# First loads issued one behind another, the bias product moved behind the first chunk, and the rotated score products of a head pair put in one group

## The chip, the cores and the metric

One Trainium2 chip, one of its cores. The metric is the device time of one execution in microseconds (us), as the median of several runs. The work is in fp32 accuracy: each fp32 weight tile is cut into a high and a low part, and each product of the large layers is done as three products of parts.

## The reference

Two transformer blocks over 256 tokens of width 1024. What matters here is the very start and the first attention, a latent attention (MLA) with 8 heads:

```python
h = x @ w_in                                  # 384 query, 256 key/value, 64 rotary columns
c_q  = _rmsnorm(h[..., :384], g_q)
c_kv = _rmsnorm(h[..., 384:640], g_kv)
k_r = _rope(h[..., 640:], pos)
q = einsum('bsr,rhd->bshd', c_q, w_uq)
q_n, q_r = q[..., :128], _rope(q[..., 128:], pos)
...
s = (q_n . k_n  +  q_r . k_r) * scale         # causal, per head; 128 plus 64 deep
p = softmax(s)
...
```

The second attention (sliding window, 16 heads of depth 64) adds a relative bias to its scores. After it come MLPs, a recurrence, a stick-breaking attention, a memory attention and a convolutional FFN. They are not touched.

## The kernel before

The program is written out by hand for each engine, with semaphores between them.

All large weights come as one stream of 319 slots of 512 KB. SyncE (SP) loads slot n into `raw[:, n % 4]`. ScalarE makes the high part `whi` (line 1472), VectorE subtracts to get the low part `wlo` (line 2093), and TensorE uses both. A `raw` buffer is loaded anew when its `wlo` is made (`cut_lo`). ScalarE and VectorE cut three slots ahead of TensorE (`AHEAD = 3`): slots 0, 1 and 2 before the loop, and slot j + 3 at the head of its turn j.

At the start SP issues slots 0 to 3 without a wait. ScalarE issues from its own queue, in this order: the first two of eight feature chunks of x (`x_loaded`), the other six (`x_rest_loaded`), the first 1025 columns of the table `con` (identity, ones, causal mask, cosine and sine), and the parameters `par`. GpSimd issues `relb` and the band rows (`band_loaded`). Then ScalarE copies the first pair of chunks of x to `xh`, cuts slot 0, copies the other three pairs and cuts slots 1 and 2. VectorE follows with `xl` (signal `x_cut`, one count for a pair), `wlo` of slot 0, the other three pairs, and `wlo` of slots 1 and 2. Then VectorE works on `par`, reads the bias product's result (`brow`), waits for `con_loaded`, and goes on with the chunks of ("in", j).

TensorE's queue starts with 28 products of a tile of zeros, each 128 x 512 bf16. Then comes the bias product `brow` (32 deep, 16 wide, 384 columns), which waits for the band rows. Then come the chunks ("in", 0) to ("in", 2). A chunk is 8 tiles of one slot against 256 tokens, in 24 products (lines 701, 704, 705). ("in", 0) waits at tile k for `x_cut`. Then `kvstat`, ("in", 3) to ("in", 5), keys, and the list `MLA_PE`, which fixes the order of the latent attention:

```python
MLA_PE = [("g", 0), ("r", 0), ("n", 0), ("r", 1), ("n", 1), ("n", 2), ("n", 3), ("s", 0), ("s", 1), ("v", 0), ("t", 0), ("t", 1), ("s", 2),
          ("v", 1), ("t", 2), ("t", 3), ("o", 0), ("o", 1), ("s", 3), ("w", 0), ("t", 4), ("t", 5), ("w", 1), ("o", 2), ("o", 3),
```

("s", n) is the scores of heads 2n and 2n + 1. ("v", n) and ("w", n) are gathers of twelve products of 512 columns. ("t", h) is the transposes of head h's probabilities (line 926), and ("o", h) the output. For the scores, VectorE takes scaled maxima, ScalarE the exponentials, and VectorE the normalised probabilities in `sc` and `pr` (even and odd heads), line 2288. VectorE's order is scores of pair 0, normalise head 0, scores of pair 1, normalise head 1.

In ("s", n) the latent part multiplies the full height of the array (128 rows, `qn` by `kn`, line 961). The rotated part (`qr` by `kr`, line 963) is 64 deep: head 2n uses the low half of the array's rows and head 2n + 1 the high half. Query tokens 0 to 127 see keys 0 to 127 (128 columns), and tokens 128 to 255 see all 256. These operands are plain fp32, and each such product is run in two passes. The second attention's scores (line 1044) are half-height products alone: for a pair of heads 128 columns low and high, then 256 columns low and high.

The four `work` banks of PSUM are handed to results in the order of the list `RESULTS`, result n in bank n % 4.

Of the kernel before, what the change touches and what calls it, by code (L numbers as in the profile page):

```python
# [24 lines left out]
P = 128  # L25
T = 256
# [13 lines left out]
RING = 4  # L40
# [26 lines left out]
CCOL = {}  # L67
# [149 lines left out]
def _results(stage, names):  # L217
    RESULTS.extend((stage, n) for n in names)


_results("brow", [0])
_results("in", range(3))
_results("kvstat", [0])
_results("in", range(3, 6))
_results("k", range(4))
# [83 lines left out]
def build(nc, w, xt, x_tok, ln_rows, memt, mem_tok, consts_in, band_in, params_in, lora_in, gate2_in, relb_in, out):  # L309
    ctx = ExitStack()  # L310
    with ctx:
# [8 lines left out]
        raw = tensor(ctx, "raw", [P, RING, 1024])  # L320
        whi = tensor(ctx, "whi", [P, RING, 1024], F32R)
        wlo = tensor(ctx, "wlo", [P, RING, 1024], F32R)
        con = tensor(ctx, "con", [P, NCON])
# [7 lines left out]
        xh, xl = xhl[:, 0, :, :], xhl[:, 1, :, :]  # L331
# [17 lines left out]
        with ExitStack() as first:  # L349
# [14 lines left out]
            kr = tensor(first, "kr", [P, T])  # L364
            qr = tensor(first, "qr", [P, 4, T])
            nsink = tensor(first, "nsink", [P, 16])
            qlat = tensor(first, "qlat", [P, 8, 2 * T])
            qn, kn = qlat[:, 0:4, :], qlat[:, 4:8, :]
# [54 lines left out]
        work = [ctx.enter_context(nc.psum_tensor(f"work{b}", [P, 512], F32)) for b in range(4)]  # L423
# [36 lines left out]
        def of_head(tile, h):  # L460
            return tile[:, h // 2, h % 2 * T:h % 2 * T + T]
# [81 lines left out]
        HALVES = (LOW, HIGH)  # L543
# [7 lines left out]
        raw_loaded = [sem(f"raw_loaded{r}") for r in range(RING)]  # L551
# [7 lines left out]
        def sig(name):  # L559
            if name not in named:  # L560
                named[name] = sem(name)
            return named[name]
# [27 lines left out]

        @block.sync
        def _(sp):
            for n in range(RING):
                sp.dma_start(raw[:, n, :], w[n]).then_inc(raw_loaded[n], 16)
            rounds = NSLOT // RING
            for n in range(RING, 3 * RING):
                sp.wait_ge(cut_lo, n + 1 - RING)
                sp.dma_start(raw[:, n % RING, :], w[n]).then_inc(raw_loaded[n % RING], 16)
                if n == RING + 2:
                    sp.dma_start(memraw[:, :, :], memt).then_inc(sig("mem_loaded"), 16)  # L600
                elif n == 2 * RING + 2:
                    sp.dma_start(x[:, :, :], mem_tok).then_inc(sig("mem_tok_loaded"), 16)
            with sp.Fori(3, rounds) as i:
                for r in range(RING):

                    sp.wait_ge(cut_lo, i * RING + (r + 1 - RING))
                    sp.dma_start(raw[:, r, :], w[bass.ds(i * RING + r, 1), :, :].rearrange("a p n -> p (a n)"))\
                        .then_inc(raw_loaded[r], 16)
            for n in range(rounds * RING, NSLOT):
                sp.wait_ge(cut_lo, n + 1 - RING)  # L610
                sp.dma_start(raw[:, n % RING, :], w[n]).then_inc(raw_loaded[n % RING], 16)
            for b in range(4):
                sp.wait_ge(sig("final"), b + 1)
                sp.dma_start(tok(out, b // 2, b % 2), tok(rest, b // 2, b % 2)).then_inc(sig("stored"), 16)
            sp.wait_ge(sig("stored"), 64)
# [65 lines left out]
        def _(pe):  # L681
            mm = nc.tensor.matmul
# [42 lines left out]
            def chunk(stage, j, key, hi, lo, waits=None):  # L725

                n = SLOT[stage] + j
                bank = open_result(key)
                slot_start(n)
                for k in range(DC):  # L730
                    if waits is not None:
                        waits(k)
                    last = cut_product(bank[:, 0:T], n, k, hi[:, k, :], lo[:, k, :], k == 0, k == DC - 1, k == 0)
                close_result(last, key)
# [46 lines left out]
            def zero_products(bank, count):  # L781


                for _ in range(count):
                    mm(bank[:, :], zeros[:, :], mask4(zeros[:, :]), start=True, stop=True)
# [109 lines left out]


            pe.wait_ge(sig("zeros_set"), 1)
            zero_products(work[3], 28)
            pe.wait_ge(sig("band_loaded"), 32)
            close_result(mm(open_result(("brow", 0))[0:16, 0:384], relb[:, :], bandt[:, 0, :], start=True, stop=True), ("brow", 0))  # L900
            for j in range(3):
                chunk("in", j, ("in", j), xh, xl, (lambda k: pe.wait_ge(sig("x_cut"), k // 2 + 1)) if j == 0 else None)
            pe.wait_ge(sig("con_loaded"), 16)
            bank = open_result(("kvstat", 0))
            pe.wait_ge(sig("in_sq"), 2)
            for j in range(2):
                last = mm(bank[:, 0:T], ones, hsq(j), start=j == 0, stop=j == 1)
# [4 lines left out]
            for p in range(4):  # L912
                bank = open_result(("k", p))
                for e in range(2):
                    for c in range(2):
# [3 lines left out]
                        last = cut_product(bank[:, e * T:(e + 1) * T], SLOT["uk"] + s, tile, ckvh[:, c, :], ckvl[:, c, :], c == 0, c == 1, tile == 0)  # L919
# [11 lines left out]
            for kind, n in MLA_PE:  # L931
                key = ("mla", (kind, n))
                if kind == "g":
                    bank = open_result(key)
                    pe.wait_ge(sig("in_sq"), 5)
                    for t in range(2):
                        for j in range(3):
                            last = mm(bank[:, 32 * t:32 * t + 32], hsq(2 + j)[:, half(t)], C("ones", 1).broadcast_to([P, 32]), start=j == 0, stop=j == 2)
                    close_result(last, key)
                elif kind == "v":  # L940
                    gather("v", SLOT["uv"] + n, ckvh[:, n, :], ckvl[:, n, :], n == 0, n == 1)
                elif kind in "rn":
                    bank = open_result(key)
                    for e in range(2):
                        for k in range(3):
                            s, tile = divmod(MLA_TILE[(kind, n)] + 3 * e + k, 8)
                            if tile == 0:
                                slot_start(SLOT["q"] + s)
                            last = cut_product(bank[:, e * T:(e + 1) * T], SLOT["q"] + s, tile, cqh[:, k, :], cql[:, k, :], k == 0, k == 2, tile == 0)
                    close_result(last, key)  # L950
                elif kind == "s":

                    keys = [("mla", ("s", 2 * n + e)) for e in range(2)]
                    banks = [open_result(k) for k in keys]
                    wait_drained(pe, ("k", n))
                    wait_drained(pe, ("mla", ("n", n)))
                    pe.wait_ge(sig("kr_ready"), 1)
                    pe.wait_ge(sig("qr_ready"), n // 2 + 1)
                    for cols_, q, width in ((slice(0, P), 0, P), (slice(P, 3 * P), P, T)):
                        for e, bank in enumerate(banks):  # L960
                            mm(bank[:, cols_], of_head(qn, 2 * n + e)[:, q:q + P], of_head(kn, 2 * n + e)[:, 0:width], start=True, stop=False)
                        for e, bank in enumerate(banks):
                            last = mm(bank[:, cols_], qr[HALVES[e], n, q:q + P], kr[HALVES[e], 0:width], start=False, stop=True)
                            if q:
                                close_result(last, keys[e])
                elif kind == "t":
                    transposes("mla", n, [(0, 0), (1, 1), (2, 2)])
                elif kind == "o":
                    bank = open_result(key)
                    wait_drained(pe, ("mla", ("t", n)))  # L970
                    pe.wait_ge(sig(f"v_kept{n // 4}"), 2)
                    mm(bank[:, 0:T], rest[:, 0, n * VD:(n + 1) * VD], pT[:, n % 4, 0:T], start=True, stop=False)
                    last = mm(bank[:, P:T], rest[:, 1, n * VD:(n + 1) * VD], pT[:, n % 4, T:3 * P], start=False, stop=True)
                    close_result(last, key)
                else:
                    wait_drained(pe, ("mla", ("o", n)))
                    gather("wo", SLOT["wo"] + n, oh[:, n, :], ol[:, n, :], n == 0, n == DC - 1)
# [56 lines left out]
            for kind, h in SWA_ALL:  # L1034
                key = ("swa", (kind, h))
                if kind == "s":

                    keys = [("swa", ("s", 2 * h + e)) for e in range(2)]
                    banks = [open_result(k) for k in keys]
# [11 lines left out]
                elif kind == "o":  # L1051
                    bank = open_result(key)
# [57 lines left out]
            for t in range(2):  # L1110
                bank = open_result(("vtok", t))
# [348 lines left out]
        def _(act):  # L1460
# [49 lines left out]

            act.dma_start(sqr[:, 0:2, :], xt[:, 0:2, :]).then_inc(sig("x_loaded"), 16)
            act.dma_start(sqr[:, 2:DC, :], xt[:, 2:DC, :]).then_inc(sig("x_rest_loaded"), 16)
            first_con = CCOL["blockones"]
            act.dma_start(con[:, 0:first_con], consts_in[:, 0:first_con]).then_inc(sig("con_loaded"), 16)
            act.dma_start(par[:, :], params_in).then_inc(sig("par_loaded"), 16)

            def table(func, src=None):
# [1403 lines left out]
```

## Time and profile before

| | us |
|---|---|
| median of 3 runs | 1075.38 (1075.04 to 1075.98) |
| the profiled execution | 1074.92 |
| its span | 1073.1 |
| TensorE busy with products | 1063.8 |
| VectorE busy | 781.5 |
| ScalarE busy | 642.5 |

The span runs from the first to the last instruction of the profile; 1.8 us of the execution lie around it. Times of instructions are counted from the span's start. Products (PE) are pipelined and their ends are modelled, so the distance between two starts says more than one duration. PEld is the loading of weights into the array, DVE is VectorE, ACT is ScalarE, and SPq, ACTq and POOLq are the issuing of transfers. The time to landing of a transfer counts from its issue.

### The profile page before, as it was taken

The page shows a single profiled execution, that of the slowest core. Times are in us where ns is not written, and L with a number is a line of the kernel's source. Part 1 is how long each engine was busy: PE and PEld are TensorE (multiplying, and loading weights), DVE is VectorE, ACT ScalarE, POOL GpSimd, SP SyncE. Part 2 cuts the span into 40 slices and gives each one's busy share as a digit, 9 for nine tenths or more (in the row PEclk, how much of TensorE's full clock was granted, in tenths as well). Part 3 has the DMA queues.
Part 4 walks back from the last instruction along what each step waited for, and adds up shares of the span by engine and source line. Part 5 has one row for each costly group of instructions (what it writes and reads, how often), then busy time and mean ns, then how long its engine had stood idle before and what let it go on. Part 6 is the DMA issues. An engine that isn't in the chain of part 4 may idle for free.

```text
span 1073.1 us, 21320 instructions
## 1 busy us (share of the span) xinstructions
PE 1063.8 (99%) x7745; PEld 931.8 (87%) x7745; DVE 781.5 (73%) x1370; ACT 642.5 (60%) x1160; POOL 15.0 (1%) x29
## 2 busy tenths in 40 slices
PE   9999999999999999999999999999999999999998
PEld 7978888888887788888888988898999979999997
DVE  5877766667896676666687888656764968877776
ACT  5876555544676765445568974445567357666663
POOL 1000000000000000000010000000000000000000
PEclk9999999999999999999999999999999999999999
DMA  8636555555665346555564543122255645656662
GB/s 323 248 133 216 190 184 194 195 184 170 213 216 155 103 156 197 189 182 181 190 221 135 175 136 103 49 76 76 80 177 176 180 155 178 196 180 191 183 190 97
DMA packets 49170, 181.75 MB, mean 169 GB/s; under 512 B 5537, under 2 KB 5697, under 8 KB 48209
## 3 DMA queue, kind: packets, MB, share of 16 engines
q1 hardware_dynamic: 46800, 170.41, 48.8%
q0 software_dynamic: 1584, 7.63, 2.4%
q10 hardware_dynamic: 720, 2.79, 0.7%
q8 instruction: 46, 0.75, 0.3%
q14 instruction: 20, 0.16, 0.1%
HBM read 179.74 MB, written 1.07 MB: 168 GB/s over the span
## 4 chain that ended last, share of the span: by engine, by line
PE 86%; DVE 8%; ACT 3%; issue 1%; DMA 1%; ACTq 0%; DVEq 0%
PE acc L774 25%; PE work L717 8%; PE work L701 7%; PE work L704 7%; PE work L705 7%; PE work L720 4%; PE acc L701 4%; PE acc L705 3%; PE acc L704 3%; DVE wlo L2093 3%; ACT whi L1472 2%; PE work L722 1%; PE work L757 1%; DMA sqr<-x_t 1%; PE work L926 1%
## 5 line engine op out<-in xcount | busy, mean ns | idle before, releaser
L2093 DVE TENSOR_TENSOR wlo<-raw,whi 128x1024 fp32r<-128x1024 f32 x317 | 382.5, 1223 | 87.1 <-ACT whi L1472 85.2
L1472 ACT ACTIVATE whi<-raw 128x1024 fp32r<-128x1024 f32 x319 | 335.4, 1058 | 50.1 <-PE work L701 18.9
L701 PE MATMUL work<-xhl,whi 128*128 128x256 f32 x544 | 154.4, 284 | 0.9 <-ACT k_ L1818 0.2
L704 PE MATMUL work<-xhl,whi 128*128 128x256 f32 x544 | 152.7, 281 | 0.0
L705 PE MATMUL work<-xhl,wlo 128*128 128x256 f32 x544 | 152.7, 281 | 0.0
L717 PE MATMUL work<-xhl,whi 128*128 128x512 f32 x420 | 148.9, 393 | 0.0
L720 PE MATMUL work<-xhl,wlo 128*128 128x256 f32 x480 | 124.7, 280 | 0.0
L774 PE MATMUL acc<-whi,hh 128*128 128x512 f32 x344 | 109.6, 396 | 0.7 <-DVE hl L2108 0.7
L774 PE MATMUL acc<-whi,hl 128*128 128x512 f32 x344 | 109.0, 395 | 0.0
L774 PE MATMUL acc<-wlo,hh 128*128 128x512 f32 x344 | 108.9, 395 | 0.0
L701 PEld LDWEIGHTS work<-xhl,whi 128*128 128x128 f32 x544 | 102.5, 188 | 5.4 <-DVE sm L2272 1.6
L704 PEld LDWEIGHTS work<-xhl,whi 128*128 128x128 f32 x544 | 102.5, 188 | 1.1 <-issue 0.2
L705 PEld LDWEIGHTS work<-xhl,wlo 128*128 128x128 f32 x544 | 102.6, 189 | 0.0
L720 PEld LDWEIGHTS work<-xhl,wlo 128*128 128x128 f32 x480 | 90.4, 188 | 5.0
L717 PEld LDWEIGHTS work<-xhl,whi 128*128 128x128 f32 x420 | 78.9, 188 | 17.9
L701 PE MATMUL acc<-xhl,whi 128*128 128x256 f32 x288 | 86.2, 299 | 0.0
L1712 ACT ACTIVATE ha<-work 128x256 f32<-128x256 f32 x64 | 24.6, 384 | 94.3 <-PE work L717 91.6
L704 PE MATMUL acc<-xhl,whi 128*128 128x256 f32 x288 | 80.8, 281 | 0.0
L705 PE MATMUL acc<-xhl,wlo 128*128 128x256 f32 x288 | 80.8, 281 | 0.0
L774 PEld LDWEIGHTS acc<-wlo,hh 128*128 128x128 f32 x344 | 64.5, 187 | 15.8
L774 PEld LDWEIGHTS acc<-whi,hl 128*128 128x128 f32 x344 | 64.5, 188 | 15.6
L774 PEld LDWEIGHTS acc<-whi,hh 128*128 128x128 f32 x344 | 63.3, 188 | 12.7 <-DVE hl L2108 1.5
(464 smaller groups left out, 1900.5 us busy)
## 6 DMA issues: line engine op xcount, KB each, us to landing
raw<-weights SPq DMA_DIRECT2D x319, 512.0 KB, 3.7
gb<-ln_rows POOLq DMA_DIRECT2D x4, 1024.0 KB, 6.7
memraw<-mem_t SPq DMA_DIRECT2D x1, 1024.0 KB, 7.2
x<-mem_tok SPq DMA_DIRECT2D x1, 1024.0 KB, 5.8
x<-x_tok ACTq DMA_DIRECT2D x1, 1024.0 KB, 6.6
qlat<-bias_scratch POOLq DMA_DIRECT2D x1, 1024.0 KB, 11.1
qlat<-bias_scratch POOLq DMA_DIRECT2D x4, 256.0 KB, 4.3
out_tok<-res SPq DMA_DIRECT2D x4, 256.0 KB, 2.1
```

Source lines behind the costliest of these rows:

```text
L701: a = mm(dst, whi[:, n % RING, col], hi, start=start, stop=False, skip_group_check=shared)
L704: mm(dst, whi[:, n % RING, col], lo, start=False, stop=False, skip_group_check=shared)
L705: return mm(dst, wlo[:, n % RING, col], hi, start=False, stop=stop, skip_group_check=shared)
L717: a = mm(two_halves(bank), whi[:, n % RING, col], xhl[:, :, k, :], **both)
L720: last = mm(bank[:, 0:T], wlo[:, n % RING, col], xh[:, k, :], start=False, stop=False, skip_group_check=True)
L722: last = mm(two_halves(bank), whi[:, n % RING, col], xhl[:, :, k, :], **both)
L757: last = mm(banks[j][:, 0:T], whi[:, (n + j) % RING, k * P:k * P + P], xl[:, k, :], start=False, stop=k == DC - 1)
L774: ins = mm(acc[2 * t + d][:, :], left[:, half(t)], right[:, n % RING, d * 512:d * 512 + 512], start=first and a == 0, stop=last and a == 2)
L926: last = nc.tensor.transpose(bank[:, b * P:b * P + P], probability_buffer(stage, h)[:, a * P:a * P + P], C("ident"))
L1472: act_fn(whi[:, n % RING, :], raw[:, n % RING, :], ACT.Copy).then_inc(cut_hi, 1)
L1712: act_fn(ha[:, f % 2, :], bank[:, T:2 * T] if f >= 2 or it is not None else bank[:, 0:T], ACT.Copy).then_inc(sig("up_low"), 1)
L2093: tt(wlo[:, n % RING, :], raw[:, n % RING, :], whi[:, n % RING, :].bitcast(F32), ALU.subtract).then_inc(cut_lo, 1)
```

## The change

- SP issues slot 0 at once, slot 1 when the first part of x has landed, slot 2 when the rest of x has landed, slot 3 when slot 1 has landed, and then, when slot 2 has landed, the first columns of `con`, which ScalarE issued before.
- TensorE runs 31 products of zeros instead of 28, and the bias product comes behind ("in", 0) instead of ahead of it. The list of results follows, so ("in", 0) has bank 0 and the bias product bank 1.
- In the latent scores of a head pair the four latent products come first (head by head, 128 then 256 columns), and the four rotated products stand together behind them. The first product of a bank starts it, and those of its other columns don't.

```diff
-_results("brow", [0])
-_results("in", range(3))
+_results("in", [0])
+_results("brow", [0])
+_results("in", range(1, 3))
...
-            for n in range(RING):
-                sp.dma_start(raw[:, n, :], w[n]).then_inc(raw_loaded[n], 16)
+            sp.dma_start(raw[:, 0, :], w[0]).then_inc(raw_loaded[0], 16)
+            sp.wait_ge(sig("x_loaded"), 16)
+            sp.dma_start(raw[:, 1, :], w[1]).then_inc(raw_loaded[1], 16)
+            sp.wait_ge(sig("x_rest_loaded"), 16)
+            sp.dma_start(raw[:, 2, :], w[2]).then_inc(raw_loaded[2], 16)
+            sp.wait_ge(raw_loaded[1], 16)
+            sp.dma_start(raw[:, 3, :], w[3]).then_inc(raw_loaded[3], 16)
+            sp.wait_ge(raw_loaded[2], 16)
+            first_con = CCOL["blockones"]
+            sp.dma_start(con[:, 0:first_con], consts_in[:, 0:first_con]).then_inc(sig("con_loaded"), 16)
...
-            zero_products(work[3], 28)
+            zero_products(work[3], 31)
+            chunk("in", 0, ("in", 0), xh, xl, lambda k: pe.wait_ge(sig("x_cut"), k // 2 + 1))
             pe.wait_ge(sig("band_loaded"), 32)
             close_result(mm(open_result(("brow", 0))[0:16, 0:384], relb[:, :], bandt[:, 0, :], start=True, stop=True), ("brow", 0))
-            for j in range(3):
-                chunk("in", j, ("in", j), xh, xl, (lambda k: pe.wait_ge(sig("x_cut"), k // 2 + 1)) if j == 0 else None)
+            for j in range(1, 3):
+                chunk("in", j, ("in", j), xh, xl)
...
-                    for cols_, q, width in ((slice(0, P), 0, P), (slice(P, 3 * P), P, T)):
+                    tiles = ((slice(0, P), 0, P), (slice(P, 3 * P), P, T))
+                    for e, bank in enumerate(banks):
+                        for cols_, q, width in tiles:
+                            mm(bank[:, cols_], of_head(qn, 2 * n + e)[:, q:q + P], of_head(kn, 2 * n + e)[:, 0:width], start=q == 0, stop=False,
+                               skip_group_check=True)
+                    for cols_, q, width in tiles:
                         for e, bank in enumerate(banks):
-                            mm(bank[:, cols_], of_head(qn, 2 * n + e)[:, q:q + P], of_head(kn, 2 * n + e)[:, 0:width], start=True, stop=False)
-                        for e, bank in enumerate(banks):
-                            last = mm(bank[:, cols_], qr[HALVES[e], n, q:q + P], kr[HALVES[e], 0:width], start=False, stop=True)
+                            last = mm(bank[:, cols_], qr[HALVES[e], n, q:q + P], kr[HALVES[e], 0:width], start=False, stop=q > 0,
+                                      skip_group_check=True)
                             if q:
                                 close_result(last, keys[e])
...
-            first_con = CCOL["blockones"]
-            act.dma_start(con[:, 0:first_con], consts_in[:, 0:first_con]).then_inc(sig("con_loaded"), 16)
             act.dma_start(par[:, :], params_in).then_inc(sig("par_loaded"), 16)
```

## Rows read from the trace of the kernel before

**Rows 1.** The page's busy time, share of the span and instructions.
```profile
PE 1063.8 (99%) x7745; PEld 931.8 (87%) x7745; DVE 781.5 (73%) x1370; ACT 642.5 (60%) x1160; POOL 15.0 (1%) x29
```

**Rows 2.** TensorE's waits from 0 to 100 us: total, times, longest.
```profile
PE work L701 <- DVE wlo L2093: 0.2, 1, 0.2
```

**Rows 3.** Chain that ended last, first 60 us: start, us, what.
```profile
1.19 9.13 DMA sqr<-x_t
10.34 1.67 ACT xhl L1585 x3
12.02 0.96 ACT whi L1472
...
14.28 0.38 PE work L701
```

**Rows 4.** Timeline of TensorE's weight loads, first 11 us: start, duration, instruction.
```profile
1.41 0.15 PEld L785 LDWEIGHTS work<-zeros 128*128 128x128 bf16 x1 [0.28 <-issue]
...
6.50 2.90 PEld L785 LDWEIGHTS work<-zeros 128*128 128x128 bf16 x14 [0.25 <-issue]
9.91 0.11 PEld L900 LDWEIGHTS work<-qlat,relb 32*16 32x16 f32 x2 [0.50 <-DMA qlat<-band_rows]
10.65 0.19 PEld L701 LDWEIGHTS work<-xhl,whi 128*128 128x128 f32 x1 [0.64 <-issue]
```

**Rows 5.** Timeline of TensorE's products, from 8.5 us and to 17.3 us.
```profile
8.23 1.67 PE L785 MATMUL work<-zeros 128*128 128x512 bf16 x7
...
13.86 0.28 PE L705 MATMUL work<-xhl,wlo 128*128 128x256 f32 x1
...
17.21 0.28 PE L701 MATMUL work<-xhl,whi 128*128 128x256 f32 x1
```

**Rows 6.** Timeline of VectorE, first 13 us.
```profile
7.99 1.23 DVE L2093 TENSOR_TENSOR wlo<-raw,whi 128x1024 fp32r<-128x1024 f32 x1 [0.25 <-ACT whi L1472]
11.01 1.89 DVE L2108 TENSOR_TENSOR xhl<-sqr,xhl 128x512 fp32r<-128x512 f32 x3 [1.79 <-ACT xhl L1585]
```

**Rows 7.** Windows: busy of each engine, then PEclk, DMA share, GB/s.
```profile
1.00:8.00 7.00, 6.99 (x20) 2.63 (x21) 0.70 (x2) 3.07 (x4) 1.29 (x4) 1.00 0.86 271
```

**Rows 8.** Transfers: issued near 0.7, near 2.4 and near 14.3 us.
```profile
sqr<-x_t ACTq DMA_DIRECT2D x1, 256.0 KB, 5.5
...
raw<-weights SPq DMA_DIRECT2D x1, 512.0 KB, 12.0
...
raw<-weights SPq DMA_DIRECT2D x1, 512.0 KB, 3.5
```

**Rows 9.** TensorE's products of ("s", 0), merged and in narrow stretches.
```profile
49.14 0.60 PE L961 MATMUL work<-qlat 128*128 128x128 f32 x4
49.47 0.28 PE L961 MATMUL work<-qlat 128*128 128x128 f32 x1
49.68 0.49 PE L963 MATMUL work<-kr,qr 64*128 64x128 f32 x4
49.89 0.28 PE L963 MATMUL work<-kr,qr 64*128 64x128 f32 x2
...
51.79 0.71 PE L961 MATMUL work<-qlat 128*128 128x128 f32 x4
```

**Rows 10.** TensorE's products of the second attention's first score group.
```profile
310.07 0.93 PE L1044 MATMUL work<-ks,qlat 64*128 64x128 f32 x8
310.93 0.39 PE L701 MATMUL work<-xhl,whi 128*128 128x256 f32 x1
```

**Rows 11.** Timelines of ScalarE, VectorE and the weight loads, 51 to 58 us.
```profile
51.66 1.28 ACT L1644 ACT_TABLE_LOAD   x1 [0.42 <-ACT x L1667]
...
52.81 0.16 DVE L2278 TENSOR_TENSOR sm<-sm,cols 128x2 f32<-128x2 f32 x1
...
57.02 0.35 DVE L2288 TENSOR_SCALAR pr<-pr,sm 128x256 f32<-128x256 f32 x1
...
57.67 0.14 PEld L926 LDWEIGHTS work<-con,pr 128*128 128x128 f32 x1
```

## The prediction, made blind

> **What bounds the kernel now.** I read the page first: TensorE is busy 1063.8 us of a span of 1073.1 [rows 1]. The reader should take from this that only two kinds of edit can pay: one that lets TensorE start its real work earlier, or one that shortens its own queue. Next I read its waits from 0 to 100 us: but for the one on the zeros tile at the very start there is one, 0.2 us for VectorE's `wlo` [rows 2]. The chain of waits tells where that comes from [rows 3]: the second transfer of x lands at 10.3, ScalarE copies it in three pieces (1.67), cuts slot 1 (0.96), VectorE subtracts it, and ("in", 1) begins at 14.28. From there the chain is TensorE alone for a long way, so its queue from 14.28 on moves as a whole: whatever makes ("in", 1) begin earlier, and whatever shortens the scores at 49 to 68 us, is kept, unless another engine has too little room behind it. Last I read single instructions around the start, the scores and the softmax.
>
> **The start, before.** The weight loads of the zero products come 0.425 us apart up to 6.10 (twelve rows from 1.41), then 14 in 2.90 us, 0.213 apart [rows 4]. 512 columns in these spacings are 1.2 and then 2.4 GHz, though the window view gives a granted clock of 1.00 [rows 7]; I go by the spacings. The last product begins at 8.23 + 6 x 0.213 = 9.51 and has streamed at 9.72 [rows 5]. The bias product waits for the band rows until 9.91 and the first weight load behind it comes at 10.65, 0.74 later [rows 4]. ("in", 0) then ends at 13.86 + 0.12 = 13.98 [rows 5]; it holds 24 products, which without a wait take 17.21 - 14.28 = 2.93 with the first load exposed, 2.82 with it hidden [rows 3, 5].
>
> **The start, after.**
> - Three more zero products: 3 x 0.213 = 0.64, all in TensorE's queue, so they end at 9.72 + 0.64 = 10.36.
> - ("in", 0) follows at once. It needs the first pair of x and `wlo` of slot 0. VectorE ends the latter at 7.99 + 1.23 = 9.22 [rows 6], from two transfers that go out as before; the zeros cover it.
> - x in full: the held loads leave 0.52 (slot 0), 1.05 (x), 0.17 (parameters) and 0.10 MB (band), 1.84 MB, in the queues. From 1 to 8 us the engines moved 7 us x 271 GB/s = 1.90 MB [rows 7], so x is in at about 8.0 instead of 10.3. ScalarE's copies run 8.0 to 9.7 [rows 3], VectorE's three subtractions behind slot 0, 1.89 in all [rows 6], 9.2 to 11.1. They are wanted at 11.1, 11.8 and 12.5, and there by 9.9, 10.5 and 11.1. No wait, where before ("in", 0) lost 13.98 - 10.65 - 2.93 = 0.40. End 10.36 + 2.82 = 13.18.
> - The bias product between two chunks: 0.74 as before plus a change of the array's shape on the way in, 0.1 (the gap at 49.6, below) = 0.84; bounds 0.74 and, with a whole change at 0.21, 0.95. ("in", 1) begins at 14.02. Nothing else waits long for this product: VectorE reaches its result after cut 2, at about 14.3, and now finds it ready at 13.9.
> - Slot 1: SP sits in its wait until the first x pair lands, 0.74 + 5.5 = 6.24 [rows 8], and issues then. The one slot load issued near 14 us, into nearly empty queues, took 3.5; the first x pair, with others beside it, 5.5 [rows 8]. I take 3.5, because only 0.7 MB is ahead of it, moving during its own start-up: in at 9.8, cut by ScalarE at 10.8 (0.96 in [rows 3]), subtracted at 12.1 (1.23 in [rows 6]); by the 5.5 in at 11.7 and subtracted at 14.0. Covered, by 1.9 us or just so.
> - Behind SP's new waits stand slots 2 and 3, the table `con` and slots 4 on. By the same 3.5: slot 2 issued 8.0, in 11.6, subtracted by 14, wanted one chunk after ("in", 1), 14.02 + 2.93 = 16.95. Slot 3 issued 9.8, in 13.3, wanted after 19.8. `con` issued 11.6, in at 15.1 (17.1 at 5.5); VectorE asks for it near 15 and TensorE near 19.8. Slot 4 is issued near 12.1, in by about 17, wanted after 22.6. Removing `con` from ScalarE's queue only brings `par` forward. All at nothing; the cover is the lead of three slots, and `con` becomes the next thing late if it lands after about 17.
>
> So ("in", 1) moves from 14.28 to 14.02: 0.26 us earlier, set by zeros, ("in", 0) and the bias product, no longer by a transfer.
>
> **The scores.** Each of four head pairs runs 2 full products of 128 columns, 2 half-height ones, 2 full of 256, 2 half-height, each in two passes. Pair 0 takes 51.79 - 49.14 = 2.65 [rows 9]. Passes stand 0.107 apart for 128 columns, 0.213 for 256. The last full pass begins at 49.47, should end at 49.58, and the half-height load comes at 49.68: 0.10 lost. Its second pass begins at 49.89 instead of 49.79: 0.11 more, the exposed load. So one change of shape costs 0.21 [rows 9]. After the change a pair has 8 full passes, 4 x 0.107 + 4 x 0.213 = 1.28, then 0.10, then one group of four half-height products of 128 and 256 columns. Such a group stands in the second attention, same shapes and order: 310.93 - 310.07 = 0.86 [rows 10]. New pair 2.24, saved 0.41, which is two changes at 0.21. Four pairs: 1.64. Nothing is added; both results of a pair close at its end as before.
>
> The Trainium skill ("TensorE: Matmul & The Clock Gate", Part 3, The mechanism) says that a weight load overlaps products in flight only when its row group differs; in the group of four the later loads meet their own half. By it three more loads to a half would be exposed, 3 x 0.107 = 0.32, and a pair would save 0.41 - 0.32 = 0.1. The rows disagree with it [rows 10]: there these loads cost nothing.
>
> **What the softmax gives back.** Before the transposes of head 1 only the gather ("v", 0) lies between them and pair 1, and both pairs are shortened: 0.82. Their load comes at 57.67; VectorE ends the probabilities at 57.02 + 0.35 = 57.37 [rows 11]; less about 0.05 for the signal, 0.25 of room. What does that row hang on? ScalarE loads its table until 51.66 + 1.28 = 52.94, and VectorE ends the scaled maximum of head 0 at 52.81 + 0.16 = 52.97 [rows 11]; the first exponential needs both: earlier scores help only by 0.05, since the table load stands behind ScalarE's own queue (the squares of `x`), which moves with the 0.26 alone. So of 0.82 only 0.30 arrives; 0.52 becomes a wait at head 1. Pairs 2 and 3 have each a whole gather and further products between them and their own transposes, and keep 0.41.
>
> **Sum.** 0.26 + 0.30 + 0.82 = 1.38 us off TensorE's queue, and so off the end: the span 1073.1 becomes 1071.7. The profiled execution took 1074.92, 1.8 more than its span and 0.5 less than the median, 1075.38; the median becomes 1074.0.
>
> **Rivals.**
> - **The softmax keeps up** (0.14): the first exponential would have to move with the scores. For it speaks that table and maximum end 0.03 apart; against, that the table comes last. 0.26 + 1.64 = 1.90: 1073.5.
> - **The fast rate comes sooner** (0.12). Zeros now set the start directly, and the step at 6.5 us is set by nothing in the code. Each us sooner saves 0.5, until slot 0 at 9.2 is the bound: at most 1.14 more. 1.38 + 1.14 = 2.5: 1072.9.
> - **The start brings nothing** (0.12): step 1 us later (0.5 lost) or the bias product at 0.95. Gain 0.8 to 1.1: 1074.3 to 1074.6.
> - **Loads of the same half are not hidden** (0.05): each pair saves 0.1, in all 0.26 + 0.4 = 0.66: 1074.7. The second attention speaks against it [rows 10]. It is what the quoted rule of the Trainium skill would give.
> - **Slot 1 late, slower** (0.07). It is issued 5 us later than before. ("in", 1) begins 2.3 after it lands (cut 0.96, subtraction 1.23, signals). The gain of the scores, 1.12, is used up when ("in", 1) begins at 15.4, slot 1 landing at 13.1, 6.9 after issue; over 0.2% slower from 15.3, 9.0 after issue. The last load of the first batch took 12.0 [rows 8]: so priced it lands at 18.2, ("in", 1) begins at 20.5, net 20.5 - 14.28 - 1.12 = 5.1, 1080.5. Against it: that one had some 4 MB around it, this 0.7.
>
> **How the numbers follow.** The forecast has 0.50, its own range 1073.5 to 1074.5. About 0.2%, 2.15 us, is what a measurement tells here from no change. Faster by more (under 1073.2): all of the sooner rate, nearly half of the softmax rival, 0.02 of the forecast, 0.20. Slower: 0.06, slot 1. Same: 0.74. Range: 1072.8 holds the sooner rate down to its bound, 1075.1 the two small-gain rivals; outside remain some 0.05 below and 0.08 above.
>
> **What would show it.** Right: no wait inside ("in", 0), x in near 8, ("in", 1) first product near 14.0, one bias product of about 0.8 ahead of it, eight half-height passes in one row of 0.9, pairs of 2.24, and a new TensorE wait of about 0.5 on VectorE's `pr` near 57. Wrong: a wait on slot 1 or x in the first 20 us, zeros whose fast spacing begins elsewhere than at 6.5, a half-height group over 1 us, or transposes of head 1 that don't wait.

## The result, and the profile after

| | before | changed |
|---|---|---|
| median of 20 runs | 1074.87 us | 1077.18 us |
| lowest to highest | 1074.54 to 1076.83 | 1074.10 to 1079.40 |
| profiled execution | 1074.92 | 1076.10 |
| its span | 1073.1 | 1074.3 |

The ratio of changed to before is 1.0014, with a 95% interval of 1.0007 to 1.0020. It goes by the means (1076.65 and 1075.11); the medians stand 2.3 us apart. The kernel became slower, and its runs spread over 5 us where those of before spread over 2. The profiled execution is one of the better half. It shows 1.2 us of the loss.

The 20 executions fall into two groups, and the granted clock tells them apart. The granted clock is TensorE's clock as a share of its full 2.4 GHz. In 8 executions its mean was 1.000, and they took 1074.10 to 1076.10 (median 1074.5, no slower than before). In the other 12 it was 0.998 or 0.996, and they took 1076.75 to 1079.40 (median 1077.8). In the executions of the kernel before that ran beside the experiments it was never under 0.999. The profiled one belongs to the first group. The fourth set of experiments below has a profile of the second kind, and shows what lowers the mean.

TensorE's waits from 0 to 100 us, for [rows 2]:

```profile
PE work L710 <- DVE ckvl L2120: 1.1, 1, 1.1
...
PE work L917 <- ACT pT L1620: 0.8, 1, 0.8
PE work L936 <- DVE pr L2300: 0.3, 1, 0.3
```

The third is the one that the prediction wanted at head 1. The first two are new and were not in it: the first key product waits for the low part of the latent, and the statistics product for ScalarE's square of ("in", 1). The chain that ended last says where the first comes from, for [rows 3]:

```profile
1.19 7.73 DMA sqr<-x_t
8.93 4.50 DMA raw<-weights
13.45 0.33 SPq L603
13.82 0.43 SPq L607
14.29 7.42 DMA raw<-weights
21.79 1.03 issue
22.82 0.38 ACT ha L1608
...
24.39 0.42 DVE ha L2231
...
30.54 0.70 DVE ckvl L2120
31.29 0.38 PE work L710
```

The reader should follow it from the top. x lands at 8.9, slot 2 is issued then and lands at 13.4, and only then does SP issue the table (L603) and the slots behind it (L607). Slot 5, issued at 14.29, lands at 21.7. ScalarE cuts it ahead of the rotation of chunk 2, VectorE's long line from there ends in `ckvl`, and TensorE waits until 31.29. ScalarE's timeline shows four waits for slots (1.63, 0.43, 2.77 and 1.36), where before it had one of 0.28:

```profile
8.94 1.68 ACT L1597 ACTIVATE xhl<-sqr 128x512 fp32r<-128x512 f32 x3 [1.02 <-DMA sqr<-x_t]
10.76 1.06 ACT L1486 ACTIVATE whi<-raw 128x1024 fp32r<-128x1024 f32 x1
13.45 1.06 ACT L1486 ACTIVATE whi<-raw 128x1024 fp32r<-128x1024 f32 x1 [1.63 <-DMA raw<-weights]
14.95 1.06 ACT L1486 ACTIVATE whi<-raw 128x1024 fp32r<-128x1024 f32 x1 [0.43 <-DMA raw<-weights]
15.91 0.36 ACT L1620 ACTIVATE pT<-work 128x256 f32<-128x256 f32 x1
19.04 1.06 ACT L1486 ACTIVATE whi<-raw 128x1024 fp32r<-128x1024 f32 x1 [2.77 <-DMA raw<-weights]
20.01 0.36 ACT L1620 ACTIVATE pT<-work 128x256 f32<-128x256 f32 x1
21.73 1.06 ACT L1486 ACTIVATE whi<-raw 128x1024 fp32r<-128x1024 f32 x1 [1.36 <-DMA raw<-weights]
```

The square at 20.01 is the one that the statistics product needs. Chunk 1 was finished near 16.8; the square stands behind the cut of slot 4, which lands at 19.0. VectorE meanwhile waits for the table, which lands at 17.8:

```profile
17.83 1.22 DVE L2105 TENSOR_TENSOR wlo<-raw,whi 128x1024 fp32r<-128x1024 f32 x1 [1.25 <-DMA con<-table]
```

The transfers, issued at 6.27 (slot 1), 10.75 (slot 3), 13.45 (table) and 13.82 (slot 4), for [rows 8]; the last number is the time to landing. Slot 2, issued at 8.93, took 4.5 too:

```profile
raw<-weights SPq DMA_DIRECT2D x1, 512.0 KB, 4.5
...
raw<-weights SPq DMA_DIRECT2D x1, 512.0 KB, 4.2
...
con<-table SPq DMA_DIRECT2D x1, 512.5 KB, 4.4
...
raw<-weights SPq DMA_DIRECT2D x1, 512.0 KB, 5.2
```

And the windows from 8 to 15 us, of before and then of the changed kernel. The last two numbers are the engines' share and GB/s:

```profile
8.00:15.00 7.00, 6.71 (x41) 4.45 (x40) 5.11 (x6) 4.38 (x6) 0.00 (x0) 1.00 0.96 367
```

```profile
8.00:15.00 7.00, 7.00 (x46) 5.10 (x45) 4.75 (x6) 3.85 (x6) 0.00 (x0) 1.00 0.76 237
```

In these 7 us the changed kernel moved 7 us x (367 - 237) GB/s = 0.9 MB less, nearly two slots. The start of TensorE's queue did improve, for [rows 4, 5]:

```profile
6.10 3.77 PEld L794 LDWEIGHTS work<-zeros 128*128 128x128 bf16 x18 [0.28 <-issue]
9.99 0.19 PEld L710 LDWEIGHTS work<-xhl,whi 128*128 128x128 f32 x1
```

```profile
13.11 0.81 PE L910 MATMUL work<-qlat,relb 32*16 32x384 f32 x2
13.86 0.39 PE L710 MATMUL work<-xhl,whi 128*128 128x256 f32 x1
```

The second chunk begins at 13.86 against 14.28. The scores, for [rows 9]:

```profile
51.20 1.47 PE L972 MATMUL work<-qlat 128*128 128x128 f32 x8
52.60 0.93 PE L976 MATMUL work<-kr,qr 64*128 64x128 f32 x8
53.46 1.58 PE L972 MATMUL work<-qlat 128*128 128x128 f32 x8
```

A pair takes 53.46 - 51.20 = 2.26. So the difference in time, changed minus before, runs like this: -0.42 at the second chunk; +0.50 at the statistics product (20.52 against 20.02); +1.96 at the first key product (31.29, 29.33); +2.06 at the scores (51.20, 49.14); +1.05 behind them (first gather of the output, 69.32 against 68.27); +1.2 at the end. The scores gave 1.0; between the second chunk and them the start took 2.5.

### The profile page after: what moved, and what is told of

Same layout as the page of the kernel before. It is cut to its first block, busy times and chain, and to the rows that moved or that the text cites. A ratio compares the mean times of both kernels' runs of the same rounds, so it can differ in the third digit from the quotient of the medians.

```text
span 1074.3 us, 21326 instructions
## 1 busy us (share of the span) xinstructions
PE 1063.1 (99%) x7748; PEld 931.8 (87%) x7748; DVE 781.7 (73%) x1370; ACT 641.2 (60%) x1160; POOL 14.9 (1%) x29
## 4 chain that ended last, share of the span: by engine, by line
PE 84%; DVE 8%; ACT 4%; DMA 2%; issue 2%; ACTq 0%; SPq 0%; DVEq 0%
PE acc L783 25%; PE work L726 8%; PE work L710 7%; PE work L713 7%; PE work L714 7%; PE work L729 4%; PE acc L710 4%; PE acc L714 3%; PE acc L713 3%; DVE wlo L2105 3%; ACT whi L1486 2%; DMA raw<-weights 1%; PE work L731 1%; PE work L766 1%; DMA sqr<-x_t 1%
## 5 line engine op out<-in xcount | busy, mean ns | idle before, releaser
L1486 ACT ACTIVATE whi<-raw 128x1024 fp32r<-128x1024 f32 x319 | 335.2, 1057 | 56.3 <-PE work L710 19.6
L726 PEld LDWEIGHTS work<-xhl,whi 128*128 128x128 f32 x420 | 78.9, 188 | 17.9
```

Of the source, the lines that this page charges most:

```text
L726: a = mm(two_halves(bank), whi[:, n % RING, col], xhl[:, :, k, :], **both)
L1486: act_fn(whi[:, n % RING, :], raw[:, n % RING, :], ACT.Copy).then_inc(cut_hi, 1)
```

## The experiments

Each kernel below was run 8 to 11 times beside the kernel before. Ratios are to that kernel, with a 95% interval.

**First set: the parts.** `free_loads` is the changed kernel with its load parts undone.

```diff
-            sp.dma_start(raw[:, 0, :], w[0]).then_inc(raw_loaded[0], 16)
-            sp.wait_ge(sig("x_loaded"), 16)
...
+            for n in range(RING):
+                sp.dma_start(raw[:, n, :], w[n]).then_inc(raw_loaded[n], 16)
...
+            act.dma_start(con[:, 0:first_con], consts_in[:, 0:first_con]).then_inc(sig("con_loaded"), 16)
```

> The changed kernel with the first loads as they were: SP issues slots 0 to 3 without a wait, and ScalarE issues the first part of the constant table. Zeros, bias product and scores stay changed. Theory 1 (the held loads run with pauses between them, the constant table lands near 18 and slot 4 at 19 instead of 13 and 15.6, and ScalarE and VectorE then stand in their queues): both new waits of TensorE are gone, at the statistics product (0.8) and at the first key product (1.1), and the time is about 1.4 below the kernel before, 1073.3 to 1073.9, with a spread between runs as small as before's (about 1). Rival (the order of the bias product and of the result banks makes the waits): they stay, and the time stays near 1076 to 1078.

Measured 1074.38 (1074.19 to 1075.52), ratio 0.9997 (0.9988 to 1.0006). Both waits are gone, so is most of the spread, and the mean granted clock is 1.000 in all 11 executions: theory 1 holds for the waits, and its rival falls. But the gain is 0.4, not 1.4, and the time lies outside the expected range. In its place a wait inside the first chunk appears:

```profile
PE work L702 <- DVE xhl L2114: 1.1, 1, 1.1
```

x lands at 10.3 as before, so the first chunk stands for it, and the bias product comes on top, behind it.

`scores_alone` is the kernel before with the third part of the change alone.

```diff
-                    for cols_, q, width in ((slice(0, P), 0, P), (slice(P, 3 * P), P, T)):
+                    tiles = ((slice(0, P), 0, P), (slice(P, 3 * P), P, T))
...
```

> The kernel before with the scores' new order alone. My step: a head pair takes 2.24 instead of 2.65, head 1's transposes wait 0.5 for VectorE, net 1.1 below the kernel before. Rival (the softmax keeps up): 1.6 below. Rival (another order of the scores costs elsewhere): no difference.

Measured 1073.79 (1073.43 to 1074.80), ratio 0.9989 (0.9980 to 0.9998): 1.0 below before, as the step had it. Its trace:

```profile
49.00 1.47 PE L962 MATMUL work<-qlat 128*128 128x128 f32 x8
...
57.31 0.52 PE L926 MATMUL work<-con,pr 128*128 128x128 f32 x3 [0.30 <-DVE pr L2292]
```

From the first score product to head 1's transposes 8.31, against 57.78 - 49.14 = 8.64 before: 0.33 of two pairs' saving arrives (predicted 0.30).

`holds_alone` is the kernel before with the held loads alone, the table by SP behind them.

> The kernel before with the held loads alone: 28 zero products, bias product ahead, scores as before. Theory 1: the two waits at the statistics product and at the first key product stand here too, the time is 1.5 to 4 above the kernel before and spreads over several us between runs. Rival (order of the bias product): within 0.5 of before.

Measured 1078.18 (1075.82 to 1080.05), ratio 1.0026 (1.0017 to 1.0036). In its profile the statistics product waits 2.5 for ScalarE, whose cut of slot 4 begins at 20.16. Behind this wait the granted clock read 0.57 from 22 to 26 us. The expected second wait, at the first key product, is not there: TensorE reaches it at 32.58 (29.33 before). The held loads with the table at their end alone make the loss and the spread; 7 of 10 executions have a mean clock of 0.998 or less.

`con_by_act` keeps slots 1 to 3 held and gives the table back to ScalarE.

```diff
-            sp.wait_ge(raw_loaded[2], 16)
-            first_con = CCOL["blockones"]
-            sp.dma_start(con[:, 0:first_con], consts_in[:, 0:first_con]).then_inc(sig("con_loaded"), 16)
...
+            act.dma_start(con[:, 0:first_con], consts_in[:, 0:first_con]).then_inc(sig("con_loaded"), 16)
```

> The changed kernel with slots 1 to 3 held, but the first part of the constant table issued by ScalarE ahead of the parameters as before. Theory 1a (the table's late landing is the main cost): most of the loss goes, about 1073.8 to 1074.5. Theory 1b (the late slots 4 and 5 cost, since ScalarE cuts them ahead of its squares): slot 4 is issued 0.4 us sooner only, x lands later, and the time stays above 1075.

Measured 1073.68 (1073.52 to 1074.49), ratio 0.9989 (0.9981 to 0.9998). One transfer's place is worth 1077.18 - 1073.68 = 3.5 us in the median, and the runs lie within 1 us again, all 11 at a mean clock of 1.000. Slot 4 is issued at 12.1 instead of 13.8, with no table ahead of it, and its cut begins at 16.48 without a wait. The price is a wait of 0.7 for slot 1, which now took 5.4 to land, near the 5.5 that the prediction had as its bound.

**Second set: the table or the slots behind it.** `con_pool_late` lets GpSimd issue the table when slot 2 has landed; SP no longer waits for that.

```diff
+            pool.wait_ge(raw_loaded[2], 16)
+            pool.dma_start(con[:, 0:first_con], consts_in[:, 0:first_con]).then_inc(sig("con_loaded"), 16)
```

> The changed kernel with the first part of the constant table issued by GpSimd instead of SP, still only when slot 2 has landed. SP no longer waits for slot 2 ahead of slot 4. Theory 1a (the table's late landing costs): it still lands near 18, VectorE waits for it ahead of cut 3, and the time stays above 1076. Theory 1b (slot 4 and 5 stand behind the wait for slot 2, and ScalarE cuts them ahead of its squares): slot 4 is issued at 11 to 12 and lands by 17, the wait at the statistics product is gone, and the time falls to 1074 or below.

Measured 1075.98 (1074.74 to 1079.29), ratio 1.0015 (1.0005 to 1.0026). The table took 6.3 in GpSimd's queue and landed at 20.0, later than in the change. Slot 4's cut begins at 16.81, and yet the statistics product, which multiplies by a column of the table, starts at 21.75, 1.7 behind the table. VectorE waited for the table ahead of cut 3:

```profile
DVE wlo L2105 <- DMA con<-table: 3.5, 1, 3.5
```

It cut slot 3 from 20.09 and copied chunk 0's result from 21.23 to 21.65. The statistics product needs that copy: it opens bank 0, which the changed order of results gave to chunk 0 (before, bank 0 held the bias product). The profile names no releaser for it, but the copy ends 0.1 ahead of it. So a late table alone delays TensorE too, by VectorE's queue, where it lands later than in the changed kernel. Theory 1a has the mechanism, though the median is 0.02 under its 1076. Theory 1b asked for 1074 or below and falls.

`slot4_late` is the other half: table early by ScalarE, SP still waiting for slot 2 ahead of slot 4.

> The changed kernel with the table issued early by ScalarE, but SP still waits for slot 2 ahead of slot 4. The other half of the pair. Theory 1a: with the table early the time is near that of the kernel with the table alone moved back, 1073.7. Theory 1b: slots 4 and 5 land at 18 to 21, the wait at the statistics product comes back, 1075 or more.

Measured 1074.07 (1073.84 to 1074.41), ratio 0.9992 (0.9983 to 1.0001). Cuts of slots 4 and 5 begin at 17.56 and 19.24; no wait at the statistics product. That is 0.4 above `con_by_act`, where theory 1b asked for 1.3 or more. SP issued slot 4 at 13.08, against 12.10 there and 13.82 in the change. So an issue 1.0 later costs little by itself. What costs is the table landing late, or 0.5 MB of table moving just ahead of slots 4 and 5.

`con_pool_early` issues the table from GpSimd when x has landed.

> The changed kernel with the table issued by GpSimd as soon as all of x has landed. Both theories: slot 1 has no rival transfer and lands near 10.8, the table near 14, slot 4 is issued near 11: no wait of TensorE in the first 50 us, in the profile the second chunk begins 0.4 or more earlier than before, time 1073.2 to 1073.5, below the 1073.7 of the kernel with the table moved back to ScalarE, which waited 0.7 for slot 1.

Measured 1076.70 (1075.02 to 1078.67), ratio 1.0013 (1.0004 to 1.0022), against my 1073.2 to 1073.5. A miss, and the same mistake as in the prediction: I gave the loads beside the table the latency that they had without it. The second chunk did begin 0.8 earlier than before, at 13.46. But slot 2, issued at 8.99 with the table at 9.26, took 7.3 us, and the third chunk waited for it:

```profile
PE work L710 <- DVE wlo L2105: 2.1, 1, 2.1
```

Behind this wait the granted clock read 0.52 from 18.7 to 22.2 us.

`squares_later` is `scores_alone` with ScalarE's two squares of memory tokens behind the exponentials of heads 3 and 5.

```diff
-MLA_ACT = [("c", 0), ("g", 0), ("r", 0), ("c", 1), ("n", 0), ("c", 2), ("r", 1), ("c", 3), ("n", 2), ("c", 4), ("q", 0), ("q", 1),
-           ("e", 0), ("e", 1), ("v", 0), ("e", 2), ("t", 0), ("t", 1), ("e", 3), ("v", 1), ("e", 4), ("V", 0), ("t", 2), ("t", 3), ("V", 1),
-           ("o", 0), ("o", 1), ("e", 5), ("w", 0), ("e", 6), ("e", 7), ("t", 4), ("t", 5), ("w", 1), ("o", 2), ("o", 3),
+MLA_ACT = [("c", 0), ("g", 0), ("r", 0), ("c", 1), ("n", 0), ("c", 2), ("r", 1), ("c", 3), ("n", 2), ("c", 4),
+           ("e", 0), ("e", 1), ("v", 0), ("e", 2), ("t", 0), ("t", 1), ("e", 3), ("q", 0), ("v", 1), ("e", 4), ("V", 0), ("t", 2), ("t", 3), ("V", 1),
+           ("o", 0), ("o", 1), ("e", 5), ("q", 1), ("w", 0), ("e", 6), ("e", 7), ("t", 4), ("t", 5), ("w", 1), ("o", 2), ("o", 3),
```

> The kernel before with the scores' new order, and ScalarE's two squares of the memory tokens moved from ahead of the first exponential to behind those of heads 3 and 5. My step: the 0.3 to 0.5 us that head 1's transposes wait hangs on ScalarE's table load behind these squares; it goes, and the time falls from 1073.8 to 1073.3. Rival (VectorE's own order, scores of pair 1 ahead of the normalisation of head 1, is what they wait for): the wait and the time stay.

Measured 1073.77 (1073.33 to 1074.46), ratio 0.9987 (0.9978 to 0.9996). The table load begins at 49.15, not at 51.66 [rows 11], the wait at head 1 is gone, and its transposes come 57.08 - 49.11 = 7.97 behind the first score product, 0.34 sooner than in `scores_alone`. So the mechanism is right, and the rival falls. But the whole is no faster (1073.77, 1073.79). In the traces the lead of 0.2 at 95 us is down to 0.05 at 309 us. Where it goes I did not find.

**Third set: a better start.** All have the new scores and the table by ScalarE. `two_first` issues slots 0 and 1 at once and 2 and 3 when x has landed.

```diff
+            for n in range(2):
+                sp.dma_start(raw[:, n, :], w[n]).then_inc(raw_loaded[n], 16)
+            sp.wait_ge(sig("x_rest_loaded"), 16)
+            for n in range(2, RING):
+                sp.dma_start(raw[:, n, :], w[n]).then_inc(raw_loaded[n], 16)
```

> The changed kernel with slots 0 and 1 issued at once, slots 2 and 3 together when all of x has landed, and the table issued by ScalarE early. Theory 1 (late table and pauses between held loads cost, and a load issued while others wait costs its 4.4 us latency only once): x in by about 9.5, slot 1 by 10.5, no wait of TensorE on slot 1 (0.7 in the kernel with the table moved back), the second chunk at 13.6 to 13.9, time 1073.0 to 1073.5. Rival (x then comes too late for the first chunk): a wait on x inside the first chunk, 1073.7 or more.

Measured 1074.24 (1073.72 to 1075.28), ratio 0.9995 (0.9986 to 1.0004). x lands at 9.9, the first chunk loses about 0.5 for it (a wait of 0.3 and the load exposed behind it), and the second begins at 14.34 instead of 13.6 to 13.9: the rival.

`two_first_bias_ahead` has the same loads, with 28 zeros and the bias product ahead of the first chunk.

> The kernel before (28 zeros, bias product ahead of the first chunk) with the scores' new order and slots 2 and 3 held until x has landed; the table by ScalarE as before. Theory: the bias product, put behind the first chunk, lies on the path at 0.75 to 0.85, while ahead of it it fills time in which the chunk would wait for x anyway; here it should begin near 9.6, the second chunk at 13.2 to 13.5, time 1072.8 to 1073.3, below the same loads with the product behind. Rival (the place of the bias product is neutral): equal to that kernel.

Measured 1073.96 (1073.13 to 1074.76), ratio 0.9989 (0.9980 to 0.9998). A miss: in the profile the zeros' fast spacing began only at 6.92, the bias product at 10.03 instead of 9.6, and the second chunk at 14.04 instead of 13.2 to 13.5. `held_bias_ahead` has that order with the loads of `con_by_act`.

> Slots 1 to 3 held as in the change, table by ScalarE, scores new, but 28 zeros and the bias product ahead. Against the kernel with the table moved back (1073.68) only the place of the bias product and three zeros differ. There the second chunk waited 0.7 for slot 1, so if slot 1 landing near 11.7 sets the second chunk, the place of the bias product is worth nothing here: 1073.5 to 1073.8. Rival (the product's place is worth 0.6 whatever the loads): 1073.1.

Measured 1074.05 (1073.43 to 1074.77), ratio 0.9992 (0.9983 to 1.0001): its rival falls, and the expected range is missed by 0.25. With these the place of the bias product can't be told from noise: 0.3 one way, 0.4 the other. Nothing beats `con_by_act` and `scores_alone`, and these two stand 0.1 apart, within their intervals: none of these starts gave anything beyond the scores that can be told from noise.

**Fourth set: which queue carries it.** `con_wait_later` is the changed kernel, but VectorE asks for the table only at the rotation of chunk 2.

```diff
-            dve.wait_ge(sig("con_loaded"), 16)
...
                 elif j == 2:
+                    dve.wait_ge(sig("con_loaded"), 16)
```

> The changed kernel, transfers as in the change, but VectorE asks for the constant table only where it uses it, at the rotation of chunk 2, and not ahead of cut 3. Theory A (VectorE's stand before cut 3 delays the chain to the first key product): the 1.1 wait there shrinks, the 0.8 at the statistics product (behind ScalarE's cut of slot 4) stays, the time falls by about 1 from 1077.2 to 1076. Theory B (ScalarE's queue, which stands at the cuts of slots 4 and 5, carries all of it): no change.

Measured 1077.60 (1074.34 to 1078.05), ratio 1.0021 (1.0011 to 1.0032): theory B, as far as so scattered runs can tell. Taking away VectorE's early wait gained nothing. The statistics product waits 2.4 for ScalarE, whose cut of slot 4 begins at 20.10:

```profile
21.58 0.76 PE L917 MATMUL work<-pT,con 128*128 128x256 f32 x1 [2.39 <-ACT pT L1620]
...
24.06 0.41 PE L710 MATMUL work<-xhl,whi 128*128 128x256 f32 x1
24.27 0.41 PE L713 MATMUL work<-xhl,whi 128*128 128x256 f32 x1
...
25.03 0.28 PE L710 MATMUL work<-xhl,whi 128*128 128x256 f32 x1
25.15 0.28 PE L713 MATMUL work<-xhl,whi 128*128 128x256 f32 x1
```

The rows behind the wait show a second price. At 24 us the products start 0.21 apart, at 25 us 0.12. The granted clock read 0.50 (1.2 GHz) from 22 to 24 us and 1.00 (2.4 GHz) from 25; its mean from 21 to 25 was 0.57, so 4 x 0.43 = 1.7 us were lost. The same 1.7 was lost behind the waits of 2.5 in `holds_alone` and 2.1 in `con_pool_early`. Some of it is won back, since the wait at the first key product goes: TensorE reaches that product at 32.51 here and at 31.29 in the profile of the change, 1.2 apart. One such stretch is 0.16% of the span, a mean clock of 0.998. Six of the eight executions here have that mean. It is 0.998 or less in 40 of the 42 executions above 1076.5 of the six kernels in which SP or GpSimd issues the table, and in no execution of a kernel in which ScalarE issues it. Why 2.1, 2.4 and 2.5 us of waiting lowered the clock in these profiles, and 2.2 in `con_pool_late` and 2.0 in the next kernel did not, the runs do not show.

`both_waits_later` also takes the squares of chunks 0 and 1 ahead of the cuts of slots 4 and 5.

```diff
                 if j < 2:
                     act_fn(hsq(j), bank[:, 0:T], ACT.Square).then_inc(sig("in_sq"), 1)
+                    cuts("in", j)
```

> As the kernel before it, and ScalarE takes the squares of chunks 0 and 1 ahead of the cuts of slots 4 and 5 instead of behind them. Theory A and B: the statistics product no longer waits for ScalarE but, if at all, for the table itself, which in some executions lands after 20; the time falls to 1074 to 1075. Rival (late slots 4 and 5 delay the copies and cuts all the same): above 1076, with the wait moved to the first key product.

Measured 1075.93 (1074.49 to 1077.66), ratio 1.0013 (1.0004 to 1.0022). The wait at the statistics product is gone; slots 4 and 5 are still cut at 20.18 and 21.64, the rotation still follows the cut of slot 5, and the first key product waits 2.0:

```profile
31.27 0.39 PE L710 MATMUL work<-ckvh,whi 128*128 128x256 f32 x1 [1.99 <-DVE ckvl L2122]
```

TensorE begins it at 31.27, as in the change (31.29), though there it had waited at the statistics product before. The medians stand 1077.60 - 1075.93 = 1.7 apart, but that is no clean price of the squares. The granted clock stays at 1.00 in this profile, and its mean is 0.998 in 4 of 11 executions here against 6 of 8 there. The median lies between the two expectations, and the rival had the mechanism.

## Why the prediction was wrong

I forecast 1074.0 in 1072.8 to 1075.1; it is 1077.18. By the prediction's own steps:

- **Three more zeros, first chunk at 10.36.** It began at 10.02. The fast spacing began at 6.10 instead of 6.50, so one product fewer ran at the slow spacing (0.2); the rest was not traced. No wait inside it; right.
- **x in at 8.0.** It landed at 8.9. Covered.
- **Bias product 0.84, second chunk at 14.02.** 13.11 to 13.86 is 0.75, plus 0.09 ahead of it; second chunk at 13.86. Right for the product. The start gained 0.42 for 0.26, and its nearness is partly luck: the first chunk began 0.34 sooner, and took 3.0 instead of 2.82.
- **Slot 1 in at 9.8.** 10.8. Covered. The rival with slot 1 late named the right kind of danger on the wrong transfer.
- **Behind SP's new waits, "All at nothing".** This is the step that failed. I priced each link at 3.5 from one row and had the table in at 15.1. The row was also misread: I wrote "nearly empty queues", but slot 4, issued at 9.25, was on its way until 15.5, and the engines moved 243 GB/s from 14.3 to 17.8. The links were 6.3 to 10.8 (slot 1), 8.9 to 13.4 (slot 2), 13.45 to 17.8 (table), each 4.4 to 4.5, and slots 4 and 5 took 5.2 and 7.4, moving behind the table and beside each other: cuts at 19.0 and 21.7. I had slot 4 "in by about 17". I even named the sign, the table "becomes the next thing late if it lands after about 17", and gave it no price and no chance. Even at 5.5 for the table I kept the cover "the lead of three slots". That lead was counted for TensorE, which needs slot 4 after 22.6. The in-order queue of ScalarE needs it much sooner: its cut stands ahead of the square that the statistics product waits for near 19.6. With slot 4 cut at 19.04 the square ends near 20.4. I looked for who waits for the slot, and not for what stands behind it on the engine that cuts it. In the profile this gave two waits, 0.8 and 1.1, that were put at nothing. The median is worse than the profile, and in 12 of 20 executions the mean granted clock was lower too, a price that the prediction had nowhere. No profile of the change itself caught that; the three profiles of other kernels that did show the fall behind a wait of TensorE.
- **The scores, 1.64 of pair time, 0.30 + 0.82 kept.** Right: 2.26 for a pair against 2.24, 1.03 against 1.12 in the medians of the kernel with them alone, and the wait at head 1 where it was said to be, 0.3 instead of 0.5. The group of four took 53.46 - 52.60 = 0.86, so the later loads of a half are hidden here too, against the rule of the Trainium skill ("TensorE: Matmul & The Clock Gate", Part 3, The mechanism) that a weight load overlaps only when its row group differs.
- **The range.** It ended at 1075.1 because the one slower rival was priced at 5 us and given 0.07. A chain of four transfers with unknown latency should have had a case of its own: at 4.5 a link the table lands at 17.9 and slot 4 at 19, and the price follows from ScalarE's queue: the statistics product began 0.5 late in the profile of the change and 1.6 late in those of `holds_alone` and `con_wait_later`, before any loss by the clock.

What is shown: the held loads with the table at their end make the loss (`holds_alone`, `free_loads`), and moving the table alone back undoes it (`con_by_act`). In the profiles of the change, `holds_alone` and `con_wait_later` the delay reaches TensorE by ScalarE's queue. By VectorE's early wait it reaches TensorE in `con_pool_late`, where the table lands at 20.0 and slot 4 in time. The slow group of executions goes with a fall of the granted clock that follows a wait of TensorE. Four profiles with the table at the end of SP's chain show slot 4's cut at 19.04, 20.10, 20.16 and 20.18; so the landing varies by over 1 us, the wait with it, and a longer wait can cost 1.7 us of clock on top. For the 12 slow executions of the change itself this is inferred from their mean clock.

Not separated: how much of the late slots 4 and 5 is the table's data ahead of them, and how much their later issue; `slot4_late` shows only that an issue 1.0 later cost 0.4 without the table in the way. Open: where the 0.3 of `squares_later` is lost, why the landings vary, and why a held load took 3.4 in one kernel and 4.9 in another.

## What to carry to other kernels

When loads are held one behind another, write the chain out with the range of latencies that loads beside others show, not with one good row of the trace, and add it up to the last link. Then look at every in-order engine that consumes the late item and list what stands behind it in its queue: the bound is set there, long before the consumer at the end needs the item. A small table that several engines need early has no place at the end of such a chain. When executions of one kernel spread, look at each one's mean granted clock: a wait of about 2 us on TensorE cost up to 1.7 us more here, in the products behind it. And a half-height group of products should stand together: each change of the array's shape cost 0.21 us here.

## What the runs showed of the hardware

- In the four profiles with the table at the end of SP's chain, slots 1 to 3 (512 KB each, with other transfers on their way) took 4.2 to 4.9 us, the table 4.4 to 5.7, slot 4 behind it 5.2 to 6.6, and slot 5 7.1 to 7.6. Slot 3 took only 3.5 in `con_by_act` and 3.4 in `slot4_late`, also with slot 2 on its way. So the number of loads on their way does not set the latency alone.
- The granted clock fell to 0.50 behind waits of TensorE of 2.1, 2.4 and 2.5 us, and each fall lost 1.7 us in all. Behind waits of 2.0 and 2.2 it did not fall.
- The zero products begin at 1.0 us in every kernel, but their fast spacing began anywhere from 3.88 to 6.92 us in the 15 profiles of this study, while the granted clock read 1.00. With 31 zeros the first chunk began between 9.3 and 10.2; at the lower end slot 0's low part, ready at about 9.2, sets it.
